# Diffusion trunk on one core: a final projection with another order of tiles, operand places and end

## The reference

```python
def out(y, z):
    y = y.reshape(y.shape[0], y.shape[1], SSD_D_INNER) * jax.nn.silu(z.astype(jnp.float32))
    return rms_norm(y, gn_w).astype(z.dtype) @ w_out     # 4096 -> 2048
...
x = x + gate * y
...
return rms_norm(x, final_norm_w)
```

## Time and profile before

| what | us |
|---|---|
| three runs | 2110.03, 2115.02, 2121.26 |
| median | 2115.02 |
| profiled execution, whole | 2120.28 |
| its span | 2118.6 |
| PE busy in the span | 2040.1 (96%) |
| DVE busy | 1452.6 (69%) |
| ACT busy | 965.4 (46%) |
| POOL busy | 693.2 (33%) |
| from the last SSD projection to the last matmul | 202.6 |
| from there to the end of the span | 13.4 |

### The profile page before, as it was taken

How to read it: one execution, slowest core, us unless ns; L and a number is a source line. 1 busy time by engine, 2 the same in 40 slices (tenths; PEclk the granted TensorE clock), 3 DMA queues, 4 the chain that set the end, 5 groups by cost and what they waited for, 6 DMA issues and landing times.

```text
span 2118.6 us, 31090 instructions
## 1 busy us (share of the span) xinstructions
PE 2040.1 (96%) x10438; PEld 1679.6 (79%) x10438; DVE 1452.6 (69%) x2019; ACT 965.4 (46%) x1387; POOL 693.2 (33%) x585
## 2 busy tenths in 40 slices
PE   5989999999999999999988999999999999999997
PEld 2558788888888888878867888888888888887776
DVE  5257777787777777864267777777877777778344
ACT  3244445445445454633354544444454444445333
POOL 1125665566565555545141111121111112111011
PEclk7999999999999999999999999999999999999999
DMA  9975666667667666654434545546455556544553
GB/s 353 371 216 134 178 181 172 159 179 185 171 170 181 174 167 164 169 144 141 122 100 128 134 129 149 135 122 163 114 144 146 133 128 158 142 120 165 221 189 139
DMA packets 417744, 349.21 MB, mean 165 GB/s; under 512 B 13504, under 2 KB 358176, under 8 KB 416544
## 3 DMA queue, kind: packets, MB, share of 16 engines
q1 hardware_dynamic: 392304, 269.76, 44.4%
q0 software_dynamic: 20400, 74.46, 14.3%
q10 hardware_dynamic: 4992, 4.37, 0.6%
HBM read 344.21 MB, written 4.33 MB: 165 GB/s over the span
## 4 chain that ended last, share of the span: by engine, by line
PE 82%; DVE 8%; DMA 4%; ACT 3%; issue 2%; POOL 1%; SPq 1%; DVEq 0%; ACTq 0%; POOLq 0%
PE bank L359 21%; PE bank L361 21%; PE bank L363 21%; DVE w_lo L344 2%; PE bank L2144 2%; PE bank L2145 2%; PE bank L2146 2%; DMA arena<-in_na_ada_w_dram 2%; PE bank L2072 1%; PE bank L2066 1%; PE bank L2056 1%; PE bank L1851 1%; DVE arena L1564 1%; DVE act_lo L1539 1%; PE bank L1877 1%
## 5 line engine op out<-in xcount | busy, mean ns | idle before, releaser
L359 PE MATMUL bank<-act_hi,w_hi 128*128 128x512 f32 (+1 forms) x2464 | 913.8, 371 | 20.4 <-DVE w_lo L344 11.0
L361 PE MATMUL bank<-act_lo,w_hi 128*128 128x512 f32 (+1 forms) x2464 | 895.4, 363 | 0.0
L363 PE MATMUL bank<-act_hi,w_lo 128*128 128x512 f32 (+1 forms) x2464 | 894.9, 363 | 0.0
L344 DVE TENSOR_TENSOR w_lo<-arena,w_hi 128x2048 fp32r<-128x2048 f32 x185 | 437.1, 2362 | 216.9 <-ACT w_hi L340 157.8
L359 PEld LDWEIGHTS bank<-act_hi,w_hi 128*128 128x128 f32 x2464 | 467.8, 190 | 109.7 <-DVE w_lo L344 18.5
L363 PEld LDWEIGHTS bank<-act_hi,w_lo 128*128 128x128 f32 x2464 | 467.5, 190 | 73.8
L361 PEld LDWEIGHTS bank<-act_lo,w_hi 128*128 128x128 f32 x2464 | 468.1, 190 | 67.7
L586 POOL TENSOR_TENSOR acc<-acc,arena 128x512 f32<-128x512 f32 x224 | 331.0, 1478 | 121.4 <-ACT arena L826 112.1
L340 ACT ACTIVATE w_hi<-arena 128x2048 fp32r<-128x2048 f32 x140 | 267.2, 1909 | 104.0 <-PE bank L2146 86.4
L1340 DVE SCALAR_TENSOR_TENSOR arena<-arena,cond_c 128x512 f32<-128x512 f32 x240 | 251.3, 1047 | 63.1 <-DMA arena<-in_ssd_ada_w_dram 41.5
L826 ACT ACTIVATE arena<-arena,cond_c 128x512 f32<-128x512 f32 x256 | 171.3, 720 | 260.9 <-POOL acc L586 152.8
(11 more groups left out here) (257 smaller groups left out, 2138.3 us busy)
## 6 DMA issues: line engine op xcount, KB each, us to landing
arena<-in_ssd_w_in_dram SPq DMA_DIRECT2D x81, 1024.0 KB, 6.0
arena<-in_na_w_in_dram SPq DMA_DIRECT2D x58, 1024.0 KB, 7.5
arena<-in_ssd_ada_w_dram POOLq DMA_DIRECT2D x96, 512.0 KB, 4.1
arena<-in_na_ada_w_dram SPq DMA_DIRECT2D x64, 512.0 KB, 8.9
arena<-in_ssd_w_out_dram SPq DMA_DIRECT2D x32, 1024.0 KB, 5.1
arena<-in_na_ada_w_dram POOLq DMA_DIRECT2D x32, 512.0 KB, 4.1
arena<-in_na_w_out_dram SPq DMA_DIRECT2D x16, 1024.0 KB, 6.3
arena<-cs_scr SPq DMA_DIRECT2D x64, 256.0 KB, 5.3
```

What stands on the lines that cost most here:

```text
L344: nc.vector.tensor_tensor(w_lo[:, n0 % 2, :], raw[slot], w_hi[:, n0 % 2, :].bitcast(F32), ALU.subtract).then_inc(s_lo, 1)
L359: nc.tensor.matmul(bank[b][:, 0:cols], hi[:, w], act_hi3[:, k, 0:cols], start=(k == 0), stop=False)
L361: nc.tensor.matmul(bank[b][:, 0:cols], hi[:, w], act_lo3[:, k, 0:cols], start=False, stop=False)
L363: mm = nc.tensor.matmul(bank[b][:, 0:cols], lo[:, w], act_hi3[:, k, 0:cols], start=False, stop=(k == KT - 1))
```

## The change

Everything up to the last group of the SSD layer stays. Then:

- **Operand places.** `y_place`: y of k 0 to 15 goes to the context half (columns 256 to 511) of the activation buffers, k 16 to 31 to the latent half. The context half is not read by the last tile of the SSD layer, the z projection, so that ACT and DVE write y of k 0 to 11 inside the last pair (`last_pair` on ACT; the branch `last` on DVE).
- **Tile order.** `OUT_TILES`: the first seven eighths of block 0 in tiles 0 to 6, the first seven of block 1 in tiles 7 to 13, then both last eighths, tiles 14 and 15, then blocks 2 and 3 as before. Block 0 goes to banks 6 and 7, block 1 to 0 and 1, 2 to 6 and 7, 3 to 0 and 1. `turn_x`, `states` and `products` of the last pair stand behind tiles 2, 7 and 10.
- **Loads.** SP asks for tiles 0 and 1 ahead of the last cs loads. The residual, gate row and final weight are loaded by SP in halves and quarters (0.5 MB each), one behind each of the loads of tiles 6 to 11, 16 and 17. POOL issues none.
- **Residual.** The transposes go in four pieces of 8, behind tiles 12, 13, 16 and 17, through banks 2 and 3.
- **The end.** Tiles 30 and 31 are multiplied first for token half 0, then for token half 1. Norm, scaling and store of half 0 come while PE works on half 1. The scaling of half 1 is split by columns between ACT and DVE, and ACT starts its own store.
- **Unrolled group.** ACT and DVE have the last group outside their loop.

```diff
+OUT_TILES = ([(0, q) for q in range(7)] + [(1, q) for q in range(7)] + [(0, 7), (1, 7)]
+             + [(m, q) for m in (2, 3) for q in range(8)])
+OUT_BANK = (6, 0, 6, 0)
...
-        y_hi3 = act_hi[:, 0:IT * LAT].rearrange("p (k t) -> p k t", k=IT)
-        y_lo3 = act_lo[:, 0:IT * LAT].rearrange("p (k t) -> p k t", k=IT)
+        def y_place(act3, k):
+
+            return act3[:, k, LAT:TOK] if k < KT else act3[:, k - KT, 0:LAT]
...
+            load_fin(0)
+            load_fin(1)
             load_cs(4 * GROUPS - 1, Turn(), 62)
...
+            for i in range(2, 32):
+                load_fin(i)
+                if 6 <= i < 10:
+                    four = slice(4 * (i - 6), 4 * (i - 6) + 4)
+                    sp.wait_ge(s_spill, 16)
+                    sp.wait_ge(s_ylo, KT)
+                    sp.dma_start(x_lat[:, four, :], x_scr[:, four, :]).then_inc(s_back, 16)
+                if i in (10, 11):
+                    cols = slice(D // 2 * (i - 10), D // 2 * (i - 9))
+                    sp.wait_ge(s_gsp, 16)
+                    sp.wait_ge(s_ylo, 24)
+                    sp.dma_start(gate_b[:, cols], gate_scr[:, cols].broadcast_to([P, D // 2])).then_inc(s_gbr, 16)
+                if i in (16, 17):
...
+                    sp.wait_ge(s_ylo, IT)
...
-            pool.dma_start(x_lat, x_scr).then_inc(s_back, 16)
-            pool.wait_ge(s_gsp, 16)
-            pool.dma_start(gate_b, gate_scr.broadcast_to([P, D])).then_inc(s_gbr, 16)
...
+            def last_pair(t1, t4, t6, t10):
+
+                evac_conv(8, 5, t10, t6)
+                fin_hi(0)
+                y_high(0, 4)
+                state_evac(2, t4)
+                y_high(4, 8)
+                z_tanh_s(3, t10)
+                fin_hi(1)
+                y_high(8, 12)
+                fin_hi(2)
+                conv_tanh(5, t6)
+                cb_by_dt(3, t1, t4)
...
-            act.wait_ge(s_used, N_OUT_S)
...
+            y_high(12, 16)
+            fin_hi(3)
+            y_high(16, 20)
+            fin_hi(4)
+            y_high(20, 24)
+            square(-2, end)
+            fin_hi(5)
+            y_high(24, 28)
+            for i in range(6, 9):
+                fin_hi(i)
+            state_evac(-1, end)
+            fin_hi(9)
+            decays(-1, end)
+            for i in range(10, 14):
+                fin_hi(i)
+            square(-1, end)
+            y_high(28, 32)
+            fin_hi(14)
...
+            for i in range(16, 32):
+                fin_hi(i)
+                if i in (17, 18):
+                    for c in range(2 * i - 30, 2 * i - 28):
+                        residual_out(c)
+                if i in (18, 20, 26):
                     for t in range(2):
...
+                        final_square((18, 20, 26).index(i), t)
...
+                    if last and j == PAIRS - 1:
+                        fin_lo(0)
+                        y_low(0, 8)
+                        fin_lo(1)
+                        conv(8, 5, 3, 4, t10, t6, lambda: fin_lo(2), x_c, x_free)
+                        return
...
+            for i in range(30):
+                if i == 7:
+                    pe.wait_ge(s_free[0], (N_OUT_S + 1) // 2)
+                    pe.wait_ge(s_free[1], N_OUT_S // 2)
+                if i == 16:
+                    pe.wait_ge(s_ofree, 2)
+                if i == 24:
+                    pe.wait_ge(s_ofree, 4)
+                out_tile(i)
+                if i == 2:
+                    turn_x(-1, end, 5, Turn(base=42))
+                if i == 7:
+                    states(-1, end, GROUPS)
+                if i == 10:
+                    products(-1, end)
+                if i in (12, 13, 16, 17):
...
+                    turn_residual(at)
+                    turn_residual(at + 1)
...
+            for t in range(2):
+                for i in (30, 31):
+                    if t == 0:
+                        pe.wait_ge(s_lo, N_OUT_S + i + 1)
+                    mm = out_product(i, t)
+                mm.then_inc(s_used, 1)
```

More of the change, by code:

```diff
@@ L1062, in hi_s, with y_high, fin_hi, ssd_group @@
                 split_hi(act, n, t10, n % 2, landed(n, t10))
-            def ssd_group(g, first):
+            def y_high(k0, k1):
+                for k in range(k0, k1):
+                    act.wait_ge(s_y, k + 1)
+                    nc.scalar.activation(y_place(act_hi3, k), y_t[:, k, :], ACT.Copy,
+                                         scale=colk[:, V_GN + k:V_GN + k + 1]).then_inc(s_yhi, 1)
+            def fin_hi(i):
+                n = N_OUT_S + i
+                split_hi(act, n, Turn(), n % 2, landed(n, Turn()))
+            def last_pair(t1, t4, t6, t10):
[10 more added lines that the diff above has]
+                cb_by_dt(3, t1, t4)
+            def ssd_group(g, first, last=False):
                 t1, t4, t6, t10 = (Turn(),) * 4 if first else (Turn(g, 1), Turn(g, 4), Turn(g, 6), Turn(g, 10))
@@ L1173, in _ @@
+            step.wait()
+            act.dma_start(out2[P:2 * P, half], x_fin[:, 1, half]).then_inc(s_out, 16)
         @block.vector
@@ new lines, in _ @@
+            y_low(12, 16)
+            combine(-2, end)
+            fin_lo(4)
+            y_low(16, 20)
+            fin_lo(5)
+            y_low(20, 24)
+            fin_lo(6)
+            y_low(24, 28)
+            fin_lo(7)
+            x_weighted(-1, end)
+            fin_lo(8)
+            decay_args(-1, end)
+            fin_lo(9)
+            cb_diagonals(-1, end)
+            for i in range(10, 13):
+                fin_lo(i)
+            combine(-1, end)
+            fin_lo(13)
+            y_low(28, 32)
@@ new lines, in _ @@
+            fin_lo(14)
+            fin_lo(15)
+            dve.wait_ge(s_ysum, 1)
+            step(nc.vector.tensor_scalar(small[:, 12:14], bank[4][:, 0:2], 1.0 / DI, EPS, ALU.mult, ALU.add))
+            step.wait()
+            nc.vector.reciprocal(small[:, 12:14], small[:, 12:14]).then_inc(s_yr0, 1)
+            dve.wait_ge(s_yr, 1)
+            done_by(0)
+            for t in range(2):
+                gated(0, t)
+            fin_lo(16)
+            for t in range(2):
+                added(0, t)
```

304 lines of the change are left out of this document (144 added, 160 removed).

## The result

The changed kernel took **2098.39 us** (median of four runs, 2098.08 to 2100.26). The kernel before, beside it, took 2115.62 (four runs, 2110.03 to 2121.26). The ratio is 0.9912, with a 95% interval of 0.99 to 0.9925: faster by 0.75 to 1.0%. Forecast were 2096.6, and the range 2089 to 2106 holds the result. Run again later (`a_same`), the changed kernel took 2098.78 beside a kernel before of 2118.44 (15 runs), ratio 0.9904 (0.9889 to 0.992). The 2115 of the first runs stood a little low, and the gain is nearer to 20 us than to 17.

The account below looks back on a forecast made before the run. The prediction took TensorE to bound the final projection, its idle time being what can be won. Savings of 13.7 us there and 4.7 in the tail, 18.4 together, from the median 2115.02 gave 2096.6 us, range 2089 to 2106.

Parts of the forecast that it names:

- The work that stays: Final projection: TensorE's tiles, last-pair matmuls, residual transposes and restarts, together 185.5 us.
- the 0.2 us of slack: Early final projection: VectorE's y pieces fit before tile 2 by only 0.2 us, tile 4 by about as little.
- rival (3): Tile loads beside residual pieces land after over 9.0 us, stalling TensorE eight times, 18.4 us, gain gone; chance 0.03.
- (a): Tile 19: residual copies and two squares ahead of ScalarE's high split make TensorE wait 0.7 us.
- (b): Tile 27: low split 26, gate, add and squares ahead of high split 27 make TensorE wait 1.0 us.
- (c): The end: with tiles 30 and 31 by token halves, TensorE waits 1.65 us for low split 31.
- 12.4 in all: Kernel before, final projection: TensorE's listed waits, 5.0 us for y, 4.9 for low weight halves, the rest smaller.
- The tail: Behind the last matmul: the end comes 8.7 us later instead of 13.4, saving 4.7 us.
- (1): Rival: VectorE and GpSimd block each other near tiles 2, 4 and 10, costing 5.5 us, 2102.2; chance 0.13.
- (2): Rival: residual pieces on SP's queue make tile loads partly late, 7 to 10 us, 2105; chance 0.05.
- (4): Rival, better: the stalls at tiles 19, 27 and the end cost little and the store 2.6 us, 2092; chance 0.05.
- (5): Rival: reordering doesn't act, tile 0's late load or y stalls remain, 5 to 8 us saved, 2108; chance 0.04.

Follow-up runs that it names:

- natural: Changed kernel with the final projection's tiles block by block again and the last pair's chain back between tiles 1 and 7: 2106.82 us.
- b_spread: Kernel before with residual and gate row loaded in six pieces, still from GpSimd, each behind a used tile: 2113.44 us.
- burst: Changed kernel with all six pieces of residual and gate row asked for at once behind tile 9's load, still from SP: 2101.63 us.
- squares: Changed kernel with ScalarE's squares of blocks 0, 1 and 2 moved one tile later, behind the next high split: 2098.49 us.
- fixes: Changed kernel with the later squares, and tile 30 multiplied whole before tile 31's two token halves: 2097.68 us.
- whole: Changed kernel with tiles 30 and 31 multiplied whole again, both token halves finished behind the last one: 2101.23 us.
- b_same: Kernel before, unchanged, profiled a second time: one execution of 2120.64 us.
- b_early: Kernel before with only the loads of final tiles 0 and 1 moved ahead of the last cs loads: 2118.14 us.
- loadlate: Changed kernel with the loads of final tiles 0 and 1 back behind the last pair's cs loads: 2102.11 us.
- best: Changed kernel with later squares, whole tile 30 before tile 31's halves, and half 0's scaling split between ScalarE and VectorE: 2097.55 us.

## Why the prediction was right, point by point

- **The work that stays, 185.5.** The stretch less its three waits is 188.45 - 3.24 = 185.2. The pace of 5.44 us for a tile and the sum of small pieces held.
- **The start.** Tile 0 was to start 1.97 us behind the last SSD projection, and it did, at 1901.75. The load was there in time, the high split ran at once behind the conv evacuation and `products` waited for nothing.
- **y at tiles 2 and 4, the 0.2 us of slack.** Tile 2's pieces were forecast 12.5 us behind that end, and the row says 1912.39, 12.6 behind. TensorE's last matmul of tile 1 and first of tile 2, with VectorE's first piece ahead of them:

```profile
1912.39 1.67 DVE L1750 SCALAR_TENSOR_TENSOR act_lo<-arena,colk,act_hi 128x256 fp32r<-128x256 f32 x4
```

```profile
1912.58 0.39 PE L2239 MATMUL bank<-w_hi,act_lo 128*128 128x512 f32 x1
1913.01 0.47 PE L2237 MATMUL bank<-w_hi,act_hi 128*128 128x512 f32 x1
```

Tile 2 started 0.43 behind the matmul before it where 0.23 is the pace, too little for a wait to be listed. The tightest point was seen rightly; the 0.2 us to spare were 0.2 us short. Ahead of it, conv's four steps took 3.11 us where they had taken 3.91. That difference was forecast as worth nothing, and at this place it indeed lay beside free time (VectorE idles 2.06 us behind it).
- **The deferral, 5.0 for y and the clock behind it.** Both are gone, as forecast, 6.7 with the fall of the clock. But `natural` has only 3.4 of waits for y, with no fall of the clock behind them, so that the parts of the change which that run keeps must have a share in the 6.7. Its other 4.7, at tile 7, stem from the order in that run.
- **The residual.** The 4.0 us wait and its 1.7 were forecast, `b_spread` gave 5.8. The pieces made no load late in the first trace: 6.5 at most, with 6.7 allowed. In `a_same` it was 7.3, and still without a wait. The bound itself was too strict, as `burst` showed: a load may come 1.17 us later still before TensorE waits, so the point from which rival (3) decides is nearer 10 us than 9.
- **The stalls left.** (a) 0.7 forecast, 0.64 measured; (b) 1.0 and 0.93; (c) 1.65 and 1.67. `squares` and `fixes` confirm their causes: without the squares ahead of the split (a) and (b) are gone, with a whole tile ahead of tile 31 (c) is gone. `whole` takes (c) as well, and no fall of the clock came with it.
- **The list of waits.** "12.4 in all" left out `turn_x`'s 0.5. Nothing in the sum hangs on it: the sum adds up the work that stays, and takes no waits off. The 1.1 us wait behind the transposes went, and no run takes the four pieces back to show that it is they.
- **The tail.** 8.7 forecast, 8.4 measured. The store was issued at 4.46 behind the last matmul where I had 4.45. It landed after 3.6 where I had 3.9. The Trainium skill (DMA: Bandwidth & Descriptors, Anatomy of one DMA) has its 2.0 us and 436 GB/s for transfers that GpSimd issues; the prediction used them for stores of SP and ScalarE, an estimate of 4.4 for both halves together. The rows say 2.6 and 3.6, issued 0.4 us apart, and decide.
- **The rivals.** (1) Collisions of VectorE and GpSimd are there, but small: the mix went to a place where it took 2.41 us instead of 3.80, four y pieces took 2.15 instead of 1.67 twice beside `add_square`, and two low splits 2.8 and 2.9 instead of 2.29. All lay in slack. (2) and (3) needed tile loads late enough to stall TensorE, and none was, up to 7.4 us. (4) wanted the stalls near nothing, and they were 3.2. (5) is out: tile 0's load was there in time, and no wait for y is left.
- **What had no term: the unrolled group.** The prediction put it at nothing, since "TensorE, which waits for neither there, hides it". TensorE did wait there, 0.33 us once in each group, and the unrolled group is 0.45 us shorter. The unrolling was not tried by itself; that it is the cause is argued from the fourteen traces.
- **What was off: the base, by 1.8 us.** 18.4 was the forecast for the saving. Stretch and tail saved 19.2, the unrolled group 0.45, together 19.65. Taken from 2115.02 this gives 2095.4, and 2098.4 was measured. The 2115.02 of three runs was low: all the later runs of the kernel before have medians of 2117.7 to 2119.1, and 2118.44 - 19.65 = 2098.8, which is what `a_same` took. So the terms held, and the miss lies in the number that they were subtracted from. That it is only 1.8 us is in part luck: a base 3.4 too low and a saving 1.25 too small work against each other. The profiled run, 5.3 above the median, had hinted at the first.

## What to carry to other kernels

Sum a change from one trace by its own stretches, and then check the result by the same stretches: here they repeat to 0.3 us, while medians of one kernel move by 3. When a chain of small steps ends later than its consumer is due, move the consumer to where other tiles can stand between, and not the chain: that was worth 3.4 us or more here, where the early loads were worth 2.3 and the free halves 1.3. And a transfer is priced by what is late behind it at its place, as 3 MB at once cost 5.8 us at one place and 2.2 at another. And two halves finished closer together can meet in their stores: with half 0's still under way, the last ones took 0.5 us longer to land.

## What the runs showed of the hardware

- **Which idle times were followed by half the clock.** The granted clock was 0.83 in a ten-microsecond piece behind waits of 3.0 us (`b_spread`, `natural`), behind 2.96 and 1.88 and behind 4.0 (before; the same two falls in `b_same` and `b_early`, there behind 3.8 and 4.2). It stayed 1.00 behind single waits of 1.67, 1.82 and 2.0 us (changed kernel, `burst`, `loadlate`), and behind 1.82 and 1.62 eight us apart (`natural`). The first wait, 3.0 us at tile 1 in all four traces of kernels that start from the one before, had the fall right behind it in `b_spread` alone; in the others it came behind the next wait. Each fall cost 1.7 us, so a wait of 3 us with a fall behind it cost nearly 5.
- **Register instructions between dependent steps.** Four conv steps take 3.44 to 3.97 us in the loop (both kernels, 1500 to 1800), and 3.11 to 3.23 in the unrolled group, once 3.76; the program is the same but for the registers in the addresses. That these are the cause was not tried by itself.
- **Stores of half the size.** 0.5 MB landed in 2.6 us (SP) and 3.6 us (ACT's queue, issued 0.4 us later), against 3.9 for 1 MB. With 1 MB issued 2.4 us ahead they took 3.2 and 4.1 (`best`), with it 2.6 us ahead 2.9 and 3.8 (`fixes`).
